# The last two experts' outputs kept in SBUF, and the gather of all other rows begun at the third last weight chunk

## What is computed

```python
def hier_moe(h, w_rg, b_rg, w_re, b_re, w_eg, w_eu, w_ed):
    ...
    gp, gi = lax.top_k(gprob, 1)
    ...
    ev, ei = lax.top_k(elog, TOP_K_INNER)
    ew = jax.nn.softmax(ev, axis=-1) * gp
    ...
    for grp in range(N_GROUPS):
        act = jax.nn.silu(jnp.einsum('nd,edf->nef', h, w_eg[grp])) * jnp.einsum('nd,edf->nef', h, w_eu[grp])
        out = out + jnp.einsum('nef,efd->nd', act * combine[:, grp, :, None], w_ed[grp])
    return out

def channel_block(h, p, ...):
    m = hier_moe(h.reshape(B * T, D), ...).reshape(B, T, D)
    pe = (p.astype(h.dtype) @ w_ple_proj) * jax.nn.sigmoid(h @ w_ple_gate)
    return layer_norm(DN_ALPHA * h + m + pe, ln2_g, ln2_b)
```

## Time and profile before

| | us |
|---|---|
| median of 3 runs | 949.62 |
| lowest and highest | 949.27, 950.83 |
| the profiled execution | 950.26 |
| its span in the profile | 948.6 |
| PE busy | 873.8 |
| DVE busy | 405.4 |
| ACT busy | 244.3 |
| POOL busy | 51.8 |

### The profile page before, as it was taken

The page is one execution under the profiler, slowest core; times in us unless marked ns, Lnnn a source line. Parts: engine busy times, 40 slices in busy tenths (PEclk is TensorE's granted clock), DMA queues, the critical chain, the costliest instruction groups (busy, mean ns, idle before and its releaser), DMA issues.

```text
span 948.6 us, 15931 instructions
## 1 busy us (share of the span) xinstructions
PE 873.8 (92%) x6438; PEld 554.7 (58%) x6438; DVE 405.4 (43%) x704; ACT 244.3 (26%) x332; POOL 51.8 (5%) x89
## 2 busy tenths in 40 slices
PE   8999999999999899889999988888989888888895
PEld 5997777889998887664444434343434343434341
DVE  6689799978967478853211101010101010101005
ACT  5441234444237532442111111111111110101110
POOL 2000000000000000000000000000000000000030
PEclk9999999999999999999999999999999999999997
DMA  8441332233333436738999999999999999999943
GB/s 310 164 173 55 132 135 92 87 134 133 134 147 106 161 136 264 310 108 329 411 423 422 423 422 423 422 423 422 423 423 423 423 423 422 423 422 423 423 155 98
DMA packets 40388, 269.89 MB, mean 285 GB/s; under 512 B 5296, under 2 KB 5568, under 8 KB 9504
## 3 DMA queue, kind: packets, MB, share of 16 engines
q1 hardware_dynamic: 35328, 252.68, 66.1%
q0 software_dynamic: 5024, 16.72, 5.1%
HBM read 258.38 MB, written 10.99 MB: 284 GB/s over the span
## 4 chain that ended last, share of the span: by engine, by line
PE 53%; DMA 35%; DVE 6%; ACT 3%; issue 2%; SPq 1%; POOLq 0%; POOL 0%; ACTq 0%; DVEq 0%
DMA raw_x<-wstream 33%; PE ps L1465 11%; PE ps L1171 7%; PE ps L1173 6%; PE ps L1172 6%; PE ps L1476 3%; PE ps L1208 2%; PE ps L1190 2%; PE ps L1209 2%; PE ps L1210 2%; PE ps L1268 2%; PE ps L1445 2%; ACT w_hi L440 1%; DVE w_lo L679 1%; PE ps L1218 1%
## 5 line engine op out<-in xcount | busy, mean ns | idle before, releaser
L1465 PE MATMUL ps<-raw_x,xs 128*64 128x512 f32 x1024 | 233.3, 596 | 48.5 <-DMA raw_x<-wstream 47.1
L1465 PEld LDWEIGHTS ps<-raw_x,xs 128*64 128x64 f32 x1024 | 78.1, 136 | 177.4 <-issue 175.3
L679 DVE TENSOR_TENSOR w_lo<-raw_dense,w_hi 128x2048 fp32r<-128x2048 f32 x44 | 101.9, 2315 | 36.0 <-ACT w_hi L440 35.9
L1476 PE MATMUL ps<-raw_x,actT 128*64 128x512 f32 x512 | 117.0, 598 | 0.0
L1108 DVE COPY actT<-ps 128x256 f32<-128x256 f32 x32 | 13.6, 425 | 239.0 <-PE ps L1483 239.0
L440 ACT ACTIVATE w_hi<-raw_dense 128x2048 fp32r<-128x2048 f32 x44 | 84.0, 1908 | 97.6 <-PE ps L1190 62.7
L811 DVE SCALAR_TENSOR_TENSOR cT_sb<-uT_sb,conv_par,cT_sb 128x350 f32<-128x350 f32 x210 | 106.8, 576 | 0.6
L1171 PE MATMUL ps<-hT_hi,w_hi 128*128 128x320 f32 x304 | 95.5, 314 | 0.2 <-issue 0.2
L1173 PE MATMUL ps<-hT_hi,w_lo 128*128 128x320 f32 x304 | 93.9, 309 | 0.0
L1172 PE MATMUL ps<-hT_lo,w_hi 128*128 128x320 f32 x304 | 93.9, 309 | 0.0
L623 ACT ACTIVATE gate_silu<-ps 64x512 f32<-64x512 f32 x32 | 19.0, 594 | 267.7 <-PE ps L1465 267.7
(11 more groups left out here) (271 smaller groups left out, 1007.5 us busy)
## 6 DMA issues: line engine op xcount, KB each, us to landing
raw_x<-wstream SPq DMA_DIRECT2D x192, 1024.0 KB, 24.6
raw_dense<-wstream SPq DMA_DIRECT2D x45, 1024.0 KB, 4.8
y_rows<-y_sb POOLq DMA_DIRECT2D x64, 128.0 KB, 5.7
ln_gb<-ln POOLq DMA_DIRECT2D x2, 1024.0 KB, 4.8
const<-consts SPq DMA_DIRECT2D x1, 1294.0 KB, 12.2
rows_sb<-x SPq DMA_DIRECT2D x2, 512.0 KB, 3.7
ln_gb<-ln_in POOLq DMA_DIRECT2D x1, 1024.0 KB, 4.9
y<-rows_sb SPq DMA_DIRECT2D x2, 512.0 KB, 2.6
```

The costliest lines, as they stand in the source:

```text
L679: tt(wlo[:, i % 2, :], raw_d[:, i % RAW_D, :], whi[:, i % 2, :].bitcast(F), ALU.subtract).then_inc(ss("lo_ready"), 1)
L1465: m = mm(ps[rows_at, 1, :], xs[:, 4 * half + k, :], w[i][:, k, :], start=half == 0 and k == 0, stop=half == 1 and k == 3)
L1476: m = mm(ps[64 * b:64 * b + 64, 4, :], aT[:, 2 * half + k, :], w[:, k, FF * b:FF * b + FF], start=half == 0 and k == 0, stop=half == 1 and ...
```

## The change

- POOL stores only the experts 0 to 29 (`STORED`). Early in the program it fills the rows of the experts 30 and 31 in `y_rows` with zeros, by two transfers from a part of `rows` that is zero, and waits for these.
- The gather no longer follows the last store. It waits for `pos_ready` and for the landing of chunk 9 of the last ring round (`raw_x_in[RAW_X - 3]`), and fetches the rows into the SBUF of ring buffers that are not used any more by then (`u`, `v`).
- The `y` of the experts 30 and 31 is copied by ACT into `y_last` (`y_keep`) and stays in SBUF.
- Gathered rows are no longer added by PE: DVE adds them, times the token's weight, to `base_rows` (`add_rows`, two passes a tile); the diagonal matrices and their products go, and so do fifteen dummy products.
- The kept `y` is added by PE: a matrix with the tokens' weights, slots by tokens, is made as rows by DVE behind expert 2 (`return_weights`), transposed by PE ahead of expert 31 (six transposes into banks 5 and 6) and copied by DVE to `backT` (`return_weights_T`). `from_kept` then multiplies it with `y_last`: four matmuls a tile, each with 64 partitions of operands, behind the two identity matmuls with the summed `base_rows`.

```diff
+LAST = 2
+STORED = EXPERTS - LAST
...
-    wdiag = Area(nc, spot["ring"], 4096).put("weight_diag", [128, TILES, 2, 128], F)
-    yg = area("split").put("y_gathered", [128, 2, TILES, D_MODEL], F)
+    y_last = a.put("y_last", [128, LAST, FF], F)
+    back = a.put("slot_weight_rows", [128, TILES, LAST, 2, SLOTS], F)
+    backT = a.put("slot_weight_cols", [128, LAST, TOK], F)
+    wlast = a.put("last_weights", [128, 3, LAST, TILES], F)
+    yg = [Area(nc, spot["u"], 16384).put("y_gathered", [128, 2, 2, D_MODEL], F),
+          Area(nc, spot["v"], 8192).put("y_gathered_last", [128, 1, 2, D_MODEL], F)]
...
-        b = (0, 2, 6)[t]
+        b = (5, 2, 0)[t]
         return ps[0:ROWS[t], b:b + 2, :].rearrange("p b c -> p (b c)")
...
-        def store_rows(n):
+        zeros = rows[64:128, 2, :]
+        pool.wait_ge(ss("wide_free"), 2)
+        for n in range(STORED, EXPERTS):
+            pool.dma_start(y_rows[n * SLOTS:(n + 1) * SLOTS, :], zeros).then_inc(ss("y_zeroed"), 16)
+        pool.wait_ge(ss("y_zeroed"), 16 * LAST)
+
+        def store_rows(n, stored):
...
-            pool.wait_ge(ss("y_stored"), n * 32 + 32)
+            pool.wait_ge(ss("y_stored"), stored * 32 + 32)
             pool.sem_inc(ss("y_free"), 1)
 
-        with pool.Fori(0, EXPERTS) as n:
-            store_rows(n)
+        with pool.Fori(0, STORED) as n:
+            store_rows(n, n)
+
         def gather_rows(count):
             pool.wait_ge(ss("pos_ready"), 1)
+            pool.wait_ge(raw_x_in[RAW_X - 3], 16 * PAIRS)
             for t in range(TILES):
                 for k in range(2):
                     pool.indirect_dma_start(
-                        out=yg[0:ROWS[t], k, t, :], out_offset=None, in_=y_rows[0:count, :],
+                        out=gathered(k, t), out_offset=None, in_=y_rows[0:count, :],
...
+        def y_keep(l):
+            act.wait_ge(ss("pe_done"), DENSE + PER_ROUND - 2 + 2 * l)
+            go(y_last[:, l, :], ps[:, 4, :], ACT.Copy).then_inc(ss("y_ready"), 1)
...
-        for t in range(TILES):
-            for k in range(2):
-                go(wdiag[:, t, k, :], ident, ACT.Identity, scale=wts[:, k, t:t + 1]).then_inc(ss("wdiag_ready"), 1)
...
+        def return_weights():
+
+            link(V.memset(base_rows[64:128, 2, :], 0.0))
+            for k in range(2):
+                for l in range(LAST):
+                    link(tt(wlast[:, k, l, :], sel[:, k, :, STORED + l], wts[:, k, :], ALU.mult))
+            link(tt(wlast[:, 2], wlast[:, 0], wlast[:, 1], ALU.add))
+            for t in range(TILES):
+                for l in range(LAST):
+                    i = ts(back[:, t, l], iota[:].unsqueeze(1).broadcast_to([128, 2, SLOTS]), rankm[:, t, STORED + l:STORED + l + 1],
+                           wlast[:, 2, l, t:t + 1], ALU.is_equal, ALU.mult)
+            i.then_inc(ss("back_ready"), 1)
+
+        def return_weights_T():
+
+            dve.wait_ge(ss("back_psum"), 1)
+            V.tensor_copy(backT[:], ps[:, 5:5 + LAST, 0:TOK]).then_inc(ss("back_T"), 1)
+
+        def add_rows(t):
+
+            dve.wait_ge(y_got[t], 32)
+            q = ROWS[t]
+            for k in range(2):
+                if k:
+                    dve.wait_ge(ss("yg_added"), t + 1)
+                stt(out=base_rows[0:q, t, :], in0=gathered(k, t), scalar=wts[0:q, k, t:t + 1], in1=base_rows[0:q, t, :],
+                    op0=ALU.mult, op1=ALU.add).then_inc(ss("base_sum" if k else "yg_added"), 1)
...
+            if first:
+                pe.wait_ge(ss("back_ready"), 1)
+                for t in range(TILES):
+                    q = ROWS[t]
+                    for l in range(LAST):
+                        m = tr(ps[:, 5 + l, 128 * t:128 * t + q], back[0:q, t, l].rearrange("p c s -> p (c s)"), ident[0:q, 0:q])
+                m.then_inc(ss("back_psum"), 1)
             expert(r, PAIRS - 1, 1, last=True)
...
-        pe.wait_ge(ss("base_ready"), TILES)
+        def from_kept(t, start, stop):
+
+            q = ROWS[t]
+            for l in range(LAST):
+                for c in range(2):
+                    m = mm(sum_psum(t)[:, 512 * c:512 * c + 512], backT[64 * c:64 * c + 64, l, 128 * t:128 * t + q],
+                           y_last[64 * c:64 * c + 64, l, :], start=start and l == 0, stop=stop and l == LAST - 1)
+            return m
+
+        pe.wait_ge(ss("back_T"), 1)
         for t in range(TILES):
             q = ROWS[t]
-            if t == 2:
-                keep_warm(WARM[8], bank=6)
+            pe.wait_ge(ss("base_sum"), t + 1)
             for c in range(2):
-                mm(sum_psum(t)[:, 512 * c:512 * c + 512], ident[0:q, 0:q], base_rows[0:q, t, 512 * c:512 * c + 512], start=True, stop=False)
-        for t in range(TILES):
...
+                mm(sum_psum(t)[:, 512 * c:512 * c + 512], ident[:, 0:q], base_rows[:, t, 512 * c:512 * c + 512], start=True, stop=False)
+            if t == 0:
+                pe.wait_ge(ss("y_ready"), EXPERTS)
+            from_kept(t, False, True).then_inc(ss("sum_psum"), 1)
```

More of the change, by code:

```diff
@@ L289, in sum_psum, with gathered @@
     def sum_psum(t):
-        b = (0, 2, 6)[t]
+        b = (5, 2, 0)[t]
         return ps[0:ROWS[t], b:b + 2, :].rearrange("p b c -> p (b c)")
+    def gathered(k, t):
+        return yg[t // 2][0:ROWS[t], t % 2, k, :]
     def rowsT_psum(t):
@@ L424, in _ @@
             with pool.Fori(EXPERTS, EXPERTS * ROUNDS) as n:
-                store_rows(n)
+                store_rows(n, n - LAST)
             gather_rows(ROUNDS * EXPERTS * SLOTS)
@@ L654, in rounds @@
             for k in range(2):
-                y_copy(r * EXPERTS + EXPERTS - 2 + k, round_start(r) + PER_ROUND - 2 + 2 * k)
+                if isinstance(r, int):
+                    y_keep(k)
+                else:
+                    y_copy(r * EXPERTS + EXPERTS - 2 + k, round_start(r) + PER_ROUND - 2 + 2 * k, LAST)
         rounds(0)
@@ L1127, in expert @@
                 alpha_h1()
+            if isinstance(r, int) and isinstance(p, int) and e == 2:
+                return_weights()
         def rounds(r):
@@ L1146, in rounds @@
             aT_copy(r * EXPERTS + EXPERTS - 2)
+            if isinstance(r, int):
+                return_weights_T()
             glu(r * EXPERTS + EXPERTS - 1)
@@ L1155, in _ @@
                 rounds(r)
+        dve.wait_ge(ss("base_ready"), TILES)
+        for t in range(TILES):
+            add_rows(t)
         def y_begin(t):
@@ L1531, in _ @@
                 rounds(r)
-        pe.wait_ge(ss("base_ready"), TILES)
+        def from_kept(t, start, stop):
[6 more added lines that the diff above has]
+        pe.wait_ge(ss("back_T"), 1)
         for t in range(TILES):
             q = ROWS[t]
-            if t == 2:
-                keep_warm(WARM[8], bank=6)
+            pe.wait_ge(ss("base_sum"), t + 1)
             for c in range(2):
-                mm(sum_psum(t)[:, 512 * c:512 * c + 512], ident[0:q, 0:q], base_rows[0:q, t, 512 * c:512 * c + 512], start=True, stop=False)
-        for t in range(TILES):
-            q = ROWS[t]
-            pe.wait_ge(ss("wdiag_ready"), 2 * t + 2)
-            pe.wait_ge(y_got[t], 32)
-            for k in range(2):
-                for c in range(2):
-                    m = mm(sum_psum(t)[:, 512 * c:512 * c + 512], wdiag[0:q, t, k, 0:q], yg[0:q, k, t, 512 * c:512 * c + 512],
-                           start=False, stop=k == 1)
-            m.then_inc(ss("sum_psum"), 1)
+                mm(sum_psum(t)[:, 512 * c:512 * c + 512], ident[:, 0:q], base_rows[:, t, 512 * c:512 * c + 512], start=True, stop=False)
+            if t == 0:
+                pe.wait_ge(ss("y_ready"), EXPERTS)
+            from_kept(t, False, True).then_inc(ss("sum_psum"), 1)
     block.__exit__(None, None, None)
```

8 lines of the change are left out of this document (4 added, 4 removed).

## The result

| | before | changed |
|---|---|---|
| median, us | 949.63 | 942.11 |
| runs (four each), lowest and highest | 949.27, 950.83 | 940.65, 942.83 |
| the profiled execution | 950.26 | 940.65 |
| its span | 948.6 | 939.0 |

The ratio is 0.9917, 95% interval 0.9899 to 0.9934. The change makes the kernel 7.5 us faster. The forecast was 935.5 with a range up to 940.2: the sign is right, the size is half of what was forecast, and the time lies above the range. Of the 6.6 us between forecast and median, 4.6 are in the profiled execution itself (span 939.0, forecast 934.4).

A forecast was written before the change was run, and what follows sets the result against it. Weight-stream bytes bound the kernel up to expert 31, then the serial end (store, gather, products, layer norm). First statistics at 917.4 plus 17.0 of layer norm gave span 934.4, 14.2 less; median 935.5, range 933.9 to 940.2.

The forecast's parts named there:

- Start of the gather: POOL's first gather, freed from the last store, was to start at 902.2 against 917.38, 15.2 us earlier.
- The gather's own length: Landings of the gathered rows at the end: tile 0 at 909.3, tile 1 at 912.3, tile 2 at 914.3.
- second rival: Gather and weights hold each other up, or POOL's way costs 2.4 us: up to 2.5 us more, 938.0; chance 0.09.
- about a us: How long gathered bytes and the last weights were to flow together, from 904.4 to about 905.3; cost taken as 0.
- DVE's additions: Adding gathered rows on DVE: 1.216 us a pass, 2.5 us a tile, all over by about 917.3.
- PE's products: Tail products on PE: 1.8 us for identity matmuls plus 1.8 for four kept ones in overlapping pairs, 3.6 a tile.
- first rival: Kept matmuls on PE run alone, without overlap: 5.4 us a tile, median 939.7; chance 0.20.
- PE isn't waited for: PE's sums at 915.4, 919.0 and 922.6 were to precede DVE's demand at 917.4, 919.3 and about 924.
- third rival: PE's granted clock falls while it idles from 910.6 to 911.8; second sum 1.3 us late, 936.8; chance 0.05.
- Costs taken as nothing elsewhere: Zero rows, `return_weights` (3.6 us on DVE), six transposes (0.8 us on PE) and DVE's result copy, each hidden: 0.
- The sum: Statistics at 917.4 plus 17.0 us of layer norm end the span at 934.4, 14.2 us less than 948.6.
- The median: Forecast 935.5 us: profiled execution 936.1, less the 0.64 by which the earlier kernel's profiled run lay above its median.

## Why the prediction was right and wrong

| step | forecast | profiled |
|---|---|---|
| first gather | 902.2 | 902.77 |
| tile 0 landed | 909.3 | 909.5 |
| tile 1 landed | 912.3 | 914.5 |
| additions end | 917.3 | 919.70 |
| sums of tiles 0, 1 | 915.4, 919.0 | 920.0, 923.8 |
| first, second statistics | 917.4, 919.3 | 920.02, 923.86 |
| end of the span | 934.4 | 939.0 |

**Start of the gather: right within 0.6.** POOL's way from the chunk's landing (901.7) to the issue was 1.1 us, and 0.7 was taken.

**The gather's own length: tile 1 was mis-sized.** The prediction put the median landing of 6.0 us behind the fourth issue. But the fourth landing was the longest of before, 7.3 behind 921.46, so it came 11.4 us behind the first issue, not 10.1: 1.3 us of the miss could have been read. Where the gather came late it was 10.8, 11.0 and 12.3; where it came early and DVE's first row of tile 1 shows the landing, 11.8, 12.8, 13.8, 12.5, 12.1 and 13.7, mean 12.8. So the early start goes with about 1.4 us more in the mean, though the two groups overlap. That fits a part of the second rival, contention, on the side of the rows and not of the weights: the last down product began at 907.24, against 906.92 in the same view of before. Both flows were there for longer than "about a us": gathered bytes from about 904.5, and weights until 906.3. The Trainium skill says in "DMA: Bandwidth & Descriptors", section "Queues, rings and completion order", that the engines go round their queues, a packet at a time; the runs agree in so far as rows gathered beside the last chunks land later in the mean, and no run separates the turns themselves.

**DVE's additions: 0.2 us too cheap in all.** A pass took 1.285, not 1.216. The nearer row was one with a scalar for each partition, as in L717 and L719, and not L1103 with a constant.

**PE's products: right but for 0.2 us a tile.** The kept products came out at 1.92 us a tile from start to start, so the pairs overlap and the first rival is false. In "TensorE: Matmul & The Clock Gate", section "Part 3: Packing small matmuls — row/col tiling", the Trainium skill gives four packed row tiles, of 32 partitions each, a gain of 3.07, and no figure for two halves; here, against an estimate of 3.6 for four one after another, they give 3.6 / 1.92 = 1.9. The changes between whole-array and half-array products do have a price, though a small one. The identity records of the kernel before follow each other every 0.43 us, as their weight loads do, so four take 1.72:

```profile
912.63 0.19 PEld L1539 LDWEIGHTS ps<-base_rows,const 128*128 128x128 f32 x1 [0.24 <-issue]
...
913.06 0.19 PEld L1539 LDWEIGHTS ps<-base_rows,const 128*128 128x128 f32 x1 [0.24 <-issue]
```

Now the groups of four start at 917.99, 919.90, 921.82 and 923.74, 1.91 or 1.92 apart: the first record behind a change and the one after it come 0.52 to 0.53 us behind their forerunners. So a tile takes 3.83 us, not 3.6.

**"PE isn't waited for": the step that failed.** It needed PE to start at 911.8. PE started at 914.65, held by a jump that the sum did not contain, and by then the clock had fallen. That is the third rival's mechanism, at a greater price (2.3 us of DVE's waits, 1.3 forecast), and with a cause in front of it that the rival lacked: it let the clock fall in an idle time of 1.2 us, and it fell in one of 3.76 and not in one of 2.47 in the run without the branch.

**Costs taken as nothing elsewhere: right.** `return_weights` fills 466.4 to 470.0 on DVE and the next copy starts at 473.21, as before. The transposes took 0.92 us at 889.91, and PE still waited 0.54 us for a chunk behind them (0.88 before). The rows of zeros went at 393.64, and the weight stream shows no loss from them: the last down product starts within 0.3 us of before.

**The sum.** Against the forecast span: +2.4 for the additions' end (0.6 start, 1.7 landing, the rest passes), +2.3 for PE, makes 4.7 of the 4.6 measured. **The median** hangs on terms that vary from run to run: the third profile of the changed kernel has a jump of 7.6 and tile 1 at 13.8, and took 943.08. The first profile, at 11.8 and 6.4, had the mildest case of both among the three of this kernel. What stays open is what makes tile 1's landing vary by 2 us between runs of one program, and what a packet that begins late waits for.

## What to carry over

A step that shortens the way to an engine must also look at what that engine's sequencer does until then: an idle time put down to "issue" at a branch is the visible end of a cost that was hidden and can grow. Put the usual way of a rare branch where it falls through, above all where transfers run at the same time; the jump that is left then stands behind the work. Where a view gives two records in one row, look at each in a stretch of its own before a number is put to either. Where landings are summed, take each transfer's own, in its place in the row, and not their median.

## What the runs showed of the hardware

- A taken jump over a large body cost PE's sequencer 3.3 to 4.9 us with idle transfer engines (nine records) and 6.0 to 7.6 us with a gather running (four); the same branch falling through cost 0.08 us in either case (six). A 16 KB packet of an "instruction" queue began 1.0 to 1.5 us into the jump without the gather and 3.1 to 4.1 us into it with the gather.
- PE idle for 3.7 to 5.1 us came back at a granted clock of 0.50 and ran four identity records in 3.4 to 3.8 us; after 2.4 us of idle time it was still at 1.00 and ran them in 1.96. The length of the idle time isn't all of it: in the kernel before the clock fell at 925.3, 0.6 us behind an idle time of 1.36.
- Four f32 products with 64 partitions each, in pairs on the two halves of the array's rows, took 1.92 us, as much as two with 128 partitions beside them. Where no product of the other kind stands next to them, two with 128 partitions took 1.72.
- The fourth of six gathers, 128 rows of 4 KB issued 1.33 us apart, landed 6.7 to 8.2 us behind its issue when the weights were through (four profiles), and 7.5 to 9.7 us behind it when the gather began beside the last chunks (ten).
